# A chain of ffn and mixer stages in split fp32: the head of the program reordered, with products of zeros on TensorE

## The reference

```python
def rmsnorm(x, g):
    x32 = x.astype(jnp.float32)
    y = x32 * lax.rsqrt(jnp.mean(x32 * x32, axis=-1, keepdims=True) + EPS)
    return (y * g.astype(jnp.float32)).astype(x.dtype)

def swiglu(h, w_in, w_out):
    gate, up = jnp.split(h @ w_in, 2, axis=-1)
    return (jax.nn.silu(gate) * up) @ w_out

x = x + 0.5 * swiglu(rmsnorm(x, norm_g[layer, 0]), ffn_w_in[layer, 0], ffn_w_out[layer, 0])
```

## Time and profile before

| | us |
|---|---|
| median of 3 runs | 2131.35 (2130.2 to 2131.36) |
| profiled execution | 2131.77 |
| its span | 2130.3 |
| TensorE busy in it | 2076.0 (97%) |
| VectorE busy | 1197.2 (56%) |
| ScalarE busy | 1029.1 (48%) |

### The profile page before, as it was taken

How to read it: one execution, slowest core, us unless ns; L and a number is a source line. 1 busy time by engine, 2 the same in 40 slices (tenths; PEclk the granted TensorE clock), 3 DMA queues, 4 the chain that set the end, 5 groups by cost and what they waited for, 6 DMA issues and landing times.

```text
span 2130.3 us, 26074 instructions
## 1 busy us (share of the span) xinstructions
PE 2076.0 (97%) x10491; PEld 1741.6 (82%) x10491; DVE 1197.2 (56%) x1542; ACT 1029.1 (48%) x1357; POOL 71.2 (3%) x113
## 2 busy tenths in 40 slices
PE   8999999999999999999999999999999999989999
PEld 6887988888888877888888879888888787877887
DVE  5445687554654566654464556654455455775454
ACT  6435436444533557654354444443455444764443
POOL 2000000000000000000000000007000000000000
PEclk9999999999999999999999999999999999999999
DMA  7553435655556342565555554677637654215553
GB/s 260 192 193 119 159 98 172 205 181 200 177 192 194 128 158 80 171 198 190 192 178 178 178 178 139 199 233 213 178 120 176 218 178 166 76 51 166 179 180 117
DMA packets 259880, 359.98 MB, mean 169 GB/s; under 512 B 19582, under 2 KB 200234, under 8 KB 259760
## 3 DMA queue, kind: packets, MB, share of 16 engines
q1 hardware_dynamic: 256800, 351.57, 50.6%
q0 software_dynamic: 2016, 4.95, 1.5%
q10 hardware_dynamic: 944, 1.79, 0.3%
HBM read 356.70 MB, written 1.57 MB: 168 GB/s over the span
## 4 chain that ended last, share of the span: by engine, by line
PE 85%; DVE 7%; ACT 5%; issue 1%; DMA 1%; DVEq 0%; ACTq 0%; SPq 0%
PE bank L421 16%; PE bank L423 16%; PE bank L422 16%; PE acc L718 6%; PE acc L719 6%; PE acc L720 6%; DVE w_lo_ L445 2%; PE bank L416 2%; PE bank L417 2%; PE bank L418 2%; ACT w_hi_ L435 2%; PE tr L699 2%; PE acc L748 1%; PE acc L750 1%; PE acc L749 1%
## 5 line engine op out<-in xcount | busy, mean ns | idle before, releaser
L445 DVE TENSOR_TENSOR w_lo_<-raw_in,w_hi_ 128x2048 fp32r<-128x2048 f32 (+1 forms) x333 | 574.8, 1734 | 217.9 <-ACT w_hi_ L435 217.6
L421 PE MATMUL bank<-w_hi_,xt_hi_ 128*128 128x512 f32 x1680 | 671.2, 400 | 7.7 <-DVE arena L1544 2.7
L423 PE MATMUL bank<-w_hi_,xt_lo_ 128*128 128x512 f32 x1680 | 656.0, 390 | 0.0
L422 PE MATMUL bank<-w_lo_,xt_hi_ 128*128 128x512 f32 x1680 | 654.7, 390 | 0.0
L435 ACT ACTIVATE w_hi_<-raw_in 128x2048 fp32r<-128x2048 f32 (+1 forms) x333 | 481.6, 1461 | 61.0 <-DMA raw_in<-ffn_w_in 32.4
L844 DVE TENSOR_TENSOR wo_lo_<-raw_out,wo_hi_ 128x2048 fp32r<-128x2048 f32 x80 | 183.8, 2297 | 483.6 <-ACT wo_hi_ L798 483.6
L421 PEld LDWEIGHTS bank<-w_hi_,xt_hi_ 128*128 128x128 f32 x1680 | 315.8, 188 | 73.4 <-issue 5.1
L423 PEld LDWEIGHTS bank<-w_hi_,xt_lo_ 128*128 128x128 f32 x1680 | 315.3, 188 | 67.6
L422 PEld LDWEIGHTS bank<-w_lo_,xt_hi_ 128*128 128x128 f32 x1680 | 316.1, 188 | 59.9
L798 ACT ACTIVATE wo_hi_<-raw_out 128x2048 fp32r<-128x2048 f32 x80 | 153.3, 1916 | 369.4 <-PE acc L720 359.4
L718 PE MATMUL acc<-wo_hi_,ht_hi_ 128*128 128x512 f32 x576 | 224.3, 389 | 2.3 <-DVE ht_lo_ L831 2.3
(11 more groups left out here) (376 smaller groups left out, 2028.8 us busy)
## 6 DMA issues: line engine op xcount, KB each, us to landing
raw_in<-ffn_w_in SPq DMA_DIRECT2D x352, 512.0 KB, 4.9
raw_out<-ffn_w_out SPq DMA_DIRECT2D x88, 1024.0 KB, 4.9
raw_in<-hg_w_in SPq DMA_DIRECT2D x16, 1024.0 KB, 5.2
raw_in<-fox_w_in SPq DMA_DIRECT2D x16, 1024.0 KB, 5.4
raw_in<-conv_w_in SPq DMA_DIRECT2D x12, 1024.0 KB, 5.2
raw_in<-hg_w_out SPq DMA_DIRECT2D x4, 1024.0 KB, 5.0
raw_in<-fox_w_out SPq DMA_DIRECT2D x4, 1024.0 KB, 5.1
raw_in<-conv_w_out SPq DMA_DIRECT2D x4, 1024.0 KB, 5.0
```

What stands on the lines that cost most here:

```text
L421: mm(o, xt_hi[:, k, tok], wh[:, par, k, 0:w], start=first, stop=False)
L422: mm(o, xt_hi[:, k, tok], wl[:, par, k, 0:w], start=False, stop=False)
L423: last = mm(o, xt_lo[:, k, tok], wh[:, par, k, 0:w], start=False, stop=end)
L445: dve.e.tensor_tensor(g.piece(g.wl, n, half, k), raw, g.piece(g.wh, n, half, k).bitcast(F32), ALU.subtract).then_inc(g.w_lo, 4 if k is Non ...
```

## The change

The head of stage 0 is written anew on every engine, and the slot is taken apart:

- **SP**: x tile 0, half 0 of chunk 0, x tile 1, half 1 of chunk 0, all on SP's queue. ScalarE's queue keeps ident and norm_g, each with a semaphore of its own.
- **TensorE**: VectorE fills `silu_` with zeros; TensorE multiplies it five times into `bank[1]` (fp32, 128 x 128 by 128 x 512), then turns tile 0 of x (which no longer waits for the gains), turns the gains, and does seven more products of zeros. Products of chunk 0 wait for the splits k by k. Tile 1 of x is turned between k = 1 and k = 2 of the first product. The other gains are turned at j = 12.
- **ScalarE**: gains, high part of tile 0, splits of chunk 0 k by k, high part of tile 1, then the splits of both halves of chunk 1 with the squares of tile 0 and of tile 1 behind a half each, the two roots, then silu of both tiles, and the remaining gains behind them.
- **VectorE**: in the same manner; it scales tile 1 between k = 3 and k = 4 of chunk 0, and splits all of chunk 1 before `rstd_`.

On TensorE, from the program's start to the first product: first before, then after. `bank<-silu_` are the products of zeros.

The diff, cut to its core:

```diff
@@ sp_program
+    def x(tile):
+        sp.e.dma_start(g.x[:, tile], g.t["x"][0, tile * P:(tile + 1) * P, :]).then_inc((g.x_in0, g.x_in1)[tile], 16)
-    chunk(0)
+    chunk(0, x)
@@ pe_product
-        pe.wait_ge(g.w_lo, 8 * n + 4 * (k // 4) + 4)
+        pe.wait_ge(g.w_lo, 8 * n + (4 * (k // 4) + 4 if n else k + 1))
@@ act_ffn (dve_ffn likewise), in the loop over chunks
+        if head and c == 0:
+            for t in range(NT):
+                read(t)
+            head()
+            continue
@@ act_begin
+    act.wait_ge(g.ident_in, 16)
+    act.step(act.e.activation(g.sums[:, 0, 4:5], g.ident[:, 0:1], ACT.Sqrt))
+    act.wait_ge(g.first_gains, 1)
+    act.e.activation(g.gains[:, 0:48], g.accs[0][:, 0:48], ACT.Copy).then_inc(g.first_gains, 1)
+    for half in range(2):
+        act_high(g, act, 0, 0, half)
+    for k in range(KT):
+        act_split(g, act, 0, k // 4, k % 4)
+    for half in range(2):
+        act_high(g, act, 0, 1, half)
     for tile in range(NT):
+        for k in range(4):
+            act_split(g, act, 1, tile, k)
+        act_squares(g, act, 0, tile)
+    for tile in range(NT):
+        act_root(g, act, 0, tile)
@@ dve_begin
+    dve.e.memset(g.silu_[:], 0.0).then_inc(g.warm, 1)
...
@@ pe_begin
+    def run_in(n):
+
+        for i in range(n):
+            pe.e.matmul(g.bank[1][:], g.silu_[:, 0, 0:P], g.silu_[:].rearrange("p a n -> p (a n)"), start=True, stop=True)
+
+    pe.wait_ge(g.warm, 1)
+    run_in(5)
+    pe.wait_ge(g.ident_in, 16)
+    for half in range(2):
+        pe_turn_half(g, pe, 0, 0, half)
+    pe.wait_ge(g.first_in, 16)
+    pe.e.transpose(g.accs[0][:, 0:48], g.gain_rows[0:48, 0, :], g.ident[0:48, 0:48]).then_inc(g.first_gains, 1)
+    run_in(7)
@@ pe_gains_slot
+    if j == 2:
+        for half in range(2):
+            pe.wait_ge(g.scaled, half + 1)
+            pe_turn_half(g, pe, 0, 1, half)
+    if j == 12:
```

More of the change, by code:

```diff
@@ L345, in sp_program, with chunk @@
 def sp_program(g, sp):
-    def chunk(n):
+    def chunk(n, front=None):
         if n == N_ALL:
@@ L350, in chunk @@
         for half in range(2):
+            if front:
+                front(half)
             sp.wait_ge(g.w_lo, 8 * (n - 1) + 4 * half + 4)
@@ L575, in act_mixer_turn_x, with act_turn_x @@
                          scale=g.gains[:, GAIN[s] + k:GAIN[s] + k + 1]).then_inc(g.xt_hi, 1)
-def act_turn_x(g, act, s, first=None):
+def act_turn_x(g, act, s):
     act.step(act.e.activation(g.sums[:, 0, 4:5], g.ident[:, 0:1], ACT.Sqrt))
@@ L686, in pe_ffn @@
     n0, u = N0[s], U[s]
-    if f != 6:
+    if f not in (0, 6):
         pe_turn_x(g, pe, s)
@@ L760, in pe_ffn, with act_ffn @@
             ins.then_inc(g.h_turned, 1)
-def act_ffn(g, act, f, slot=None, first=None, loads=None, chunks=1):
+def act_ffn(g, act, f, slot=None, head=None, loads=None, chunks=1):
     s = S_FFN[f]
@@ L768, in act_ffn @@
             act_high(g, act, s, 1, half)
-    else:
-        act_turn_x(g, act, s, first)
+    elif f:
+        act_turn_x(g, act, s)
     if loads:
@@ L817, in act_ffn, with dve_ffn @@
                          ACT.Copy).then_inc(g.ht_hi, 1)
-def dve_ffn(g, dve, f, slot=None, first=None, chunks=1):
+def dve_ffn(g, dve, f, slot=None, first=None, head=None, chunks=1):
     s = S_FFN[f]
@@ L2447, in act_begin @@
     t = g.t
[L2448 removed]
+    act.e.dma_start(g.ident[:], t["c_ident"]).then_inc(g.ident_in, 16)
     act.e.dma_start(g.gain_rows[0:48, 0, :],
                     t["norm_g"].rearrange("a b (k n) -> (a b k) n", n=P)).then_inc(g.first_in, 16)
[L2451 to L2454 removed]
@@ new lines, in act_begin, with dve_begin @@
+    for k in range(KT):
+        act_split(g, act, 0, k // 4, k % 4)
+    for half in range(2):
+        act_high(g, act, 0, 1, half)
+    for tile in range(NT):
+        for k in range(4):
[3 more added lines that the diff above has]
+        act_root(g, act, 0, tile)
+def dve_begin(g, dve):
+    dve.e.memset(g.silu_[:], 0.0).then_inc(g.warm, 1)
+    dve.wait_ge(g.first_gains, 2)
+    gain = FFN_GAIN[0]
+    for half in range(2):
+        dve_scaled(g, dve, 0, 0, half, gain)
+    for half in range(2):
+        dve_low(g, dve, 0, 0, half)
+    for k in range(4):
+        dve_split(g, dve, 0, 0, k)
+    for half in range(2):
+        dve_scaled(g, dve, 0, 1, half, gain)
+    for k in range(4):
+        dve_split(g, dve, 0, 1, k)
+    for half in range(2):
+        dve_low(g, dve, 0, 1, half)
+    for k in range(KT):
+        dve_split(g, dve, 1, k // 4, k % 4)
+    for tile in range(NT):
+        dve_ms(g, dve, 0, tile)
@@ new lines, in pe_begin @@
+def pe_begin(g, pe):
+    def run_in(n):
[4 more added lines that the diff above has]
+    pe.wait_ge(g.ident_in, 16)
+    for half in range(2):
+        pe_turn_half(g, pe, 0, 0, half)
+    pe.wait_ge(g.first_in, 16)
+    pe.e.transpose(g.accs[0][:, 0:48], g.gain_rows[0:48, 0, :], g.ident[0:48, 0:48]).then_inc(g.first_gains, 1)
+    run_in(7)
+def pe_gains_slot(g, pe, j):
+    if j == 2:
+        for half in range(2):
+            pe.wait_ge(g.scaled, half + 1)
+            pe_turn_half(g, pe, 0, 1, half)
+    if j == 12:
@@ L2469, in pe_gains_slot, with act_gains, dve_gains @@
                        g.ident[0:G_ROWS - P, 0:G_ROWS - P]).then_inc(g.other_turned, 1)
[L2472 to L2493, removed]
+def act_gains(g, act):
+    act.wait_ge(g.other_turned, 1)
+    act.e.activation(g.gains[:, 48:], g.tr[0][:, 48:G_ROWS], ACT.Copy).then_inc(g.other_gains, 1)
+    e = g.small[:, 0, 0, 0:KT]
+    act.wait_ge(g.lb_e, 1)
+    act.e.activation(e, e, ACT.Exp).then_inc(g.lb_e, 1)
+def dve_gains(g, dve):
+    dve.wait_ge(g.other_gains, 1)
+    dve.wait_ge(g.consts_in, 16 * N_CONSTS)
+    logit = g.gains[:, G_LB:G_LB + KT]
+    e, r, lb, om = g.small[:, 0, 0, 0:KT], g.small[:, 0, 1, 0:KT], g.lbs[:, 0], g.lbs[:, 1]
+    dve.e.tensor_tensor(e, logit, logit, ALU.subtract).then_inc(g.lb_e, 1)
+    dve.wait_ge(g.lb_e, 2)
+    dve.wait_ge(g.own_dve, dve.step(dve.e.reciprocal(r, e)))
+    dve.wait_ge(g.own_dve, dve.step(dve.e.tensor_tensor(e, e, r, ALU.mult)))
+    dve.wait_ge(g.own_dve, dve.step(dve.e.tensor_tensor(lb, e, e, ALU.subtract)))
+    dve.e.tensor_scalar(om, lb, -1.0, 1.0, ALU.mult, ALU.add).then_inc(g.lower_bound, 1)
 def pe_program(g, pe):
@@ L2516, in act_program @@
     act_begin(g, act)
-    act_ffn(g, act, 0, lambda j: act_gains_slot(g, act, j), first=lambda: [act_split(g, act, 0, 1, k) for k in range(4)])
+    act_ffn(g, act, 0, head=lambda: act_gains(g, act))
     act_hgrn(g, act)
@@ L2532, in dve_program @@
 def dve_program(g, dve):
[L2533 to L2536, removed]
+    dve_begin(g, dve)
+    dve_ffn(g, dve, 0, head=lambda: dve_gains(g, dve))
     dve_hgrn(g, dve)
```

12 lines of the change are left out of this document (2 added, 10 removed).

## The result

The changed kernel takes 2139.87 us (median of five runs, 2139.47 to 2142.2) against 2131.36 for the kernel before beside it (2130.2 to 2133.66): ratio 1.0040, interval 1.0029 to 1.0051. It is slower by 8.5 us, and the forecast was slower by 9.3.

What follows compares the result with a forecast made beforehand. TensorE, busy 97% of 2130.3 us, was taken to bound the kernel. Chunk 1 beginning 8.2 later, less 0.7 for a gap, plus 1.8 for the clock, gave +9.3 on 2131.35: 2140.6 us, range 2135.5 to 2144.4.

Steps and rivals of the forecast that it cites:

- The main step: Before chunk 1, TensorE stands still 5.7 us for h of tile 0, there at 33.2; otherwise it could start at 27.5.
- that sum: Load, splits, squares, roots, table load, silu, h and handing on: 12.2 us from chunk 0's split at 21.0 to 33.2.
- The price from the unsplit products of the earlier trace: Products of zeros at TensorE's start: 0.88 us each at the high clock, 1.76 at the low, taken from L2088.
- the rival of cheap zeros: At the head, a zero product costs 0.23 or 0.43 us, h still late at 28.9: +5.0, 2136.4 us; chance 7%.
- The wait at k = 4: In chunk 0's first product, TensorE waits some 0.2 us at k = 4 for the splits.
- The gap of the earlier trace: TensorE's gap at 28.44 goes, since chunk 1 is split long before: 0.7 us less.
- The clock after the stall: Behind TensorE's wait for h, 3.6 us at half speed: 1.8 us lost, bounds 0.9 and 3.4.
- The forecast's bounds: First product 14.4 to 16.5, load 5.1 to 6.8, clock 0.9 to 3.4 us: 2138.4 to 2144.4 in all.
- The sum for the head: Chunk 1 begins 8.2 us later, less 0.7 for the gap, plus 1.8 for the clock: +9.3 us.
- With no lead that could take a delay up: Behind chunk 1's start, TensorE's work is as before, so nothing absorbs the delay of +9.3 us.

Runs made afterwards that it cites:

- filled wait: The changed kernel with six more fp32 products on TensorE where it waits for h_tok, between chunk 0 and chunk 1: 2139.48 us, ratio 1.0038.
- two and three zeros: The changed kernel with squares, roots and tile 0's silu put earlier, and two and three products of zeros instead of five and seven: 2130.53 us, ratio 0.9993.

## Why the prediction was right

**The main step held.** h of tile 0 was forecast at 33.2; it was written from 32.43 and released chunk 1 at 32.97. TensorE's idle time was 5.1 against 5.7. The terms of that sum, forecast and measured: chunk 0 split at 21.0, 20.65; load 5.3, 5.6 (issued at 20.67, read from 26.29); splits 2.20, 2.10; squares 1.47, 1.37 (28.39 to 29.76); roots 0.87, 0.87; table load 1.28, 1.30; silu 0.47, 0.50; h and handing on 0.58, 0.54. The largest error, the load, was covered by an earlier split. Putting the silus earlier took 6.7 us away, and taking away the zeros alone did not.

**Zeros.** The price from the unsplit products of the earlier trace rows was right: seven from 8.82 to 14.93, 0.87 each. The five ended at 7.66, not 8.1, since the high clock was there sooner than the 6.0 that I took: 6.2 us for five are two at 1.76 and three at 0.88, a rise at about 5.0. First product at about 14.9 instead of 15.2, and at about 15.9 in the kernel with the filled wait, whose code is the same up to there: that the forecast came this close owes something to luck. That a product of zeros costs what one of data costs was the step on which the rival of cheap zeros hung, and that rival fell.

**The wait at k = 4** was 0.16, forecast 0.2. **The gap of the earlier trace rows** went, as forecast: in before, chunk 1's start to the first transposes of h_tok took 6.31, of which 0.68 is the gap, and the filled wait's 5.62 agrees with the difference.

**The clock after the stall** was mis-sized: forecast 1.8, measured 1.3. The low stretch lasted 2.9 us (32.97 to about 35.9), not 3.6. Without zeros it cost 2.0 behind the same wait. The forecast's bounds held both.

**The sum for the head.** 7.97 (32.97 less 25.00) - 0.68 + 1.29 = 8.6, and the landmark says 8.56; forecast 9.3. Of the 0.7 between them 0.2 is h and 0.5 the clock.

**"With no lead that could take a delay up"** was true of the first ffn, the mixer behind it, and the ffn behind that: the additions of 732.16 before and 740.68 after are still 8.52 apart. Behind that the two profiles drift: 7.28 at the next one (1086.41 and 1093.69), 6.60 at 1806.27 and 1812.87, 7.86 at 2125.43 and 2133.29. The code there is the same. One wait of TensorE in the third stage, before and then after, is 1.5 us shorter, which is more than the 1.24 from 8.52 to 7.28:

```profile
PE tr L1362 <- DVE wo_lo_ L1571: 4.5, 3, 3.4
```

```profile
PE tr L1375 <- DVE wo_lo_ L1584: 3.0, 3, 1.8
```

The other kernels scatter too: between the additions at 732.16 and 1086.41 there are 354.25 us in before, 353.01 in after, and 352.67 to 354.60 in the others. The stage that ends at 1806.27 took 243.47 in before, 242.78 in after, and 242.14 to 246.10 in the others. With two and three zeros it was the longest, in a profiled execution of 2133.63, well above that kernel's median. Which shift of a load or of the clock decides these waits was not tried, and stays open. That the medians differ by 8.5, just as the heads do (8.56), is in part luck: against the medians of before in the other comparisons (2131.53 to 2132.43) it would be 7.4 to 8.3.

## What to carry to other kernels

When an engine's list is reordered "in order of need", ask for each item who is waiting for it and until when. Squares, roots and silu were short and free until a load came to stand ahead of them; the next chunk needed their bank, and a split that nobody needed yet was put first. Here warming products were worth something (some 0.8 us, by one profile each) only while they ended before the data and were followed by work at once; nearly every microsecond too many was paid (2.8 of 3.2).

## What the runs showed of the hardware

- **The high clock comes at different times in the same code.** The five zeros start at 1.46 in every run; they end, by the start of the transposes, at 7.66 in after and 0.94 us later in the kernel with the filled wait. With two zeros the eight transposes behind them took 1.07 us in one run and 1.54 in another. The end of the zeros moves by some 0.9 us with it. The low stretch behind the wait for h also differs: 2.9 us in after, some 4.4 (30.96 to 35.4) without zeros.
- **The high clock was gone after a wait of 2.8 us.** In the kernel before with five zeros, the granted clock was 0.56 in the window in which that wait ended and 0.50 in the next, and the high pace came back only at 18.9.
- **The column of the granted clock is wrong at the head of a program.** It reads 1.00 for 0 to 8 us in after, where the first two zeros took 1.76 each.
- **A load asked for earlier took longer.** In the kernel with two and three zeros the first half of chunk 1 is asked for at 11.59, while loads of constants still run. By the last part of the profile's page (KB each, median us from issue to landing) its two DMAs took:

```profile
raw_in<-ffn_w_in SPq DMA_DIRECT2D x2, 512.0 KB, 7.1
```

and those of the second half in after, issued at 20.67:

```profile
raw_in<-ffn_w_in SPq DMA_DIRECT2D x2, 512.0 KB, 4.7
```

In before the same first half, asked for at 11.06, took 7.2. That the constants' loads are the reason is not shown.
